# Decoder step with gated feed-forward: seven-product up projection in 18 instead of 9 of 22 slots, all its weight sums on Pool

## The reference, cut to what matters

```python
def conv_ffn(x, buf, p, l):
    u, buf_new = causal_conv(x @ p['ffn_w_up'][l], buf, p['ffn_conv_w'][l])
    u = u + p['ffn_conv_b'][l]
    return (jax.nn.silu(u[..., :D_FF]) * u[..., D_FF:]) @ p['ffn_w_down'][l], buf_new
```

## Time and profile before

| | |
|---|---|
| median of 3 runs | 2889.76 us (2887.61 to 2890.92) |
| the profiled execution | 2890.29 us |
| its span | 2888.6 us |
| PE busy | 2756.4 us, 95% |
| DVE busy | 1524.4 us, 53% |
| ACT busy | 1024.2 us, 35% |
| Pool busy | 477.7 us, 17% |
| mean TensorE clock granted | 0.988 of full speed |

### The profile page before, as it was taken

One profiled execution on the slowest core, in us unless ns is written; L12 is line 12 of the kernel. 1 busy time (PEld: TensorE's weight loads), 2 busy tenths in 40 slices (PEclk: granted clock), 3 DMA queues, 4 the chain that ended last, 5 costly groups with the idle time before them and its releaser, 6 DMA issues. The chain is left out here.

```text
span 2888.6 us, 58689 instructions
## 1 busy us (share of the span) xinstructions
PE 2756.4 (95%) x22859; PEld 2195.5 (76%) x22859; DVE 1524.4 (53%) x3221; ACT 1024.2 (35%) x3105; POOL 477.7 (17%) x605
## 2 busy tenths in 40 slices
PE   7999999999999999999999899899998999999998
PEld 4779768898766667898766777668895679867887
DVE  7665547642243327753542565337726875537661
ACT  2233234522432224431655344325412133324431
POOL 0000110063213210054100002110161000110044
PEclk9999999999999999999999999999999999999998
DMA  5420124434333223343433004533442330123442
GB/s 155 155 75 6 40 71 146 132 127 116 87 108 91 72 78 119 130 132 116 138 104 109 6 6 122 162 113 128 132 137 77 122 105 6 27 68 121 131 136 78
DMA packets 356654, 287.82 MB, mean 100 GB/s; under 512 B 74700, under 2 KB 352764, under 8 KB 355996
## 3 DMA queue, kind: packets, MB, share of 16 engines
q1 hardware_dynamic: 337456, 267.03, 30.1%
q10 hardware_dynamic: 14828, 14.93, 1.6%
q0 software_dynamic: 4096, 2.11, 0.4%
HBM read 263.29 MB, written 20.73 MB: 98 GB/s over the span
## 5 line engine op out<-in xcount | busy, mean ns | idle before, releaser
L362 PE MATMUL bank<-h,weights 128*128 128x320 f32 (+2 forms) x3152 | 788.6, 408 | 8.1 <-ACT h L447 8.1
L362 PEld LDWEIGHTS bank<-h,weights 128*128 128x128 f32 (+1 forms) x3152 | 567.9, 189 | 217.3 <-issue 17.1
L362 PE MATMUL bank<-arena,weights 128*128 128x320 f32 (+5 forms) x3088 | 663.3, 375 | 12.2 <-DVE arena L1407 6.6
L362 PE MATMUL bank<-arena 128*128 128x160 f32 (+7 forms) x5034 | 640.1, 291 | 12.3 <-DVE arena L2745 5.1
L362 PEld LDWEIGHTS bank<-arena,weights 128*128 128x128 f32 (+2 forms) x3088 | 505.4, 188 | 153.3 <-issue 23.0
L362 PEld LDWEIGHTS bank<-arena 128*128 128x128 f32 (+2 forms) x5034 | 543.7, 171 | 37.1 <-issue 14.5
L571 POOL TENSOR_TENSOR arena<-weights 128x512 f32<-128x512 f32 (+1 forms) x48 | 58.2, 1212 | 726.6 <-DMA weights<-ffn_w_down 630.6
L362 PE MATMUL bank<-h,arena 64*64 64x64 f32 (+3 forms) x3000 | 174.4, 232 | 2.6 <-DVE h L1980 1.7
L1643 POOL TENSOR_TENSOR arena<-arena,consts 128x256 f32<-128x256 f32 x30 | 22.9, 765 | 829.1 <-DVE arena L1968 583.9
L362 PEld LDWEIGHTS bank<-h,arena 64*64 64x64 f32 (+1 forms) x3000 | 151.3, 143 | 7.9 <-DVE h L1980 2.8
L894 DVE SCALAR_TENSOR_TENSOR arena<-arena,params 128x336 f32<-128x336 f32 x176 | 105.7, 601 | 68.2 <-ACT arena L754 59.4
(11 more groups left out here) (373 smaller groups left out, 3697.5 us busy)
## 6 DMA issues: line engine op xcount, KB each, us to landing
weights<-ffn_w_up SPq DMA_DIRECT2D x88, 1024.0 KB, 5.1
weights<-ffn_w_down SPq DMA_DIRECT2D x32, 1024.0 KB, 5.4
weights<-rw_wrkv SPq DMA_DIRECT2D x24, 1024.0 KB, 5.2
weights<-gdn_w_in SPq DMA_DIRECT2D x24, 1024.0 KB, 5.4
arena<-cache_mla_latent SPq DMA_DIRECT2D x108, 128.0 KB, 2.3
weights<-ffn_w_down SPq DMA_DIRECT2D x16, 768.0 KB, 4.9
weights<-rw_wo SPq DMA_DIRECT2D x8, 1024.0 KB, 5.5
weights<-gdn_wo SPq DMA_DIRECT2D x8, 1024.0 KB, 5.8
```

Of the source, the lines that this page charges most:

```text
L362: return pe.matmul(out, lhsT, rhs, start=first, stop=last, skip_group_check=True)
```

## The change

Slots 4 to 21 are all of the seven-product kind: 18 per layer instead of 9. Their weight sums all go to Pool, in front of the sums for the down projection on its queue; DVE makes none. DVE's gate is split: in even iterations the two products (L875), in odd ones, for the tiles of the iteration before, the multiplication by the sigmoid (L882 and L884 in the changed file); the HFF mixes move to the odd iterations behind it (7, 9, 15, 17 and 21; the last to 22). The waits on u2, c21 and c12 of the slot two before become waits on the slot before. In the changed file the lines have moved: L898 and L901 are the two convolution steps, L921 u2, L928 tt, L908 and L909 c22 and c12, L943 c21, L581 to L586 the mixes, L570 to L575 the weight sums.

```diff
         UP = [(c, half) for c in range(11) for half in range(2)]
-        FASTS = range(4, 21, 2)
+        FASTS = range(4, 22)
         summed = [key for l in range(layers) for key in
                   [("up", l, UP[s][1], UP[s][0]) for s in FASTS] + [("down", l, c, part) for c in range(4) for part in range(3)]]
...
 
         POOL_SUM = {"m6": "s2", "m5": "s1", "m7": "s3", "m3": "s4"}
-        DVE_SUM = {"m6": "ds2", "m5": "ds1", "m7": "ds3", "m3": "ds4"}
         MIX_FOR = {"m6": "mix2", "m5": "mix1", "m7": "mix3", "m4": "mix4"}
...
                     pe.wait_ge(*at("c22", key))
-                if step in DVE_SUM:
-                    pe.wait_ge(*at(DVE_SUM[step], key))
+                if step in POOL_SUM:
...
                     act.wait_ge(*at("m1", key))
-                    if s - 4 in FASTS:
-                        act.wait_ge(*at("u2", slot_key(l, s - 4)))
-                    act.activation(S1C[s // 2 % 2], of(("fa", key))[:, 0:HN], ACT.Copy).then_inc(*to("s1c", key))
+                    if s - 2 in FASTS:
+                        act.wait_ge(*at("u2", slot_key(l, s - 2)))
+                    act.activation(S1C[s % 2], of(("fa", key))[:, 0:HN], ACT.Copy).then_inc(*to("s1c", key))
                 if s >= 1:
...
 
         def pool_ffn(pool, l):
             pool.wait_ge(*at("rstd", 4 * l + 2))
+            for s in FASTS:
+                half_sums(pool, slot_key(l, s), POOL_SUM)
             for c in range(4):
                 for part in range(3):
...
 
-            def gate(m):
+            def gate_products(m):
 
                 g, u = CONV[:, 0, m % 2, :], CONV[:, 1, m % 2, :]
                 dve.wait_ge(*at("conv", (l, 1, m)))
-                if m:
-                    dve.wait_ge(*at("hff", (l, m - 1)))
-                dve.tensor_tensor(GD[:, 0, :], g, u, ALU.mult).then_inc(*to("gate_gu", (l, m)))
+                if m >= 2:
+                    dve.wait_ge(*at("hff", (l, m - 2)))
+                dve.tensor_tensor(GD[:, m % 2, :], g, u, ALU.mult).then_inc(*to("gate_gu", (l, m)))
+
+            def gated(m):
+
                 dve.wait_ge(*at("gate_gu", (l, m)))
                 dve.wait_ge(*at("gate_s", (l, m)))
-                s = EGATE[:, m % 2, :]
-                dve.tensor_tensor(HFF[:, m, 0:SEQ], GD[:, 0, 0:SEQ], s[:, 0:SEQ], ALU.mult)
-                win = [ap[:, 256:336].rearrange("p (b w) -> p b w", b=DEC)[:, :, 2:10] for ap in (GD[:, 0, :], s)]
+                gu, s = GD[:, m % 2, :], EGATE[:, m % 2, :]
+                dve.tensor_tensor(HFF[:, m, 0:SEQ], gu[:, 0:SEQ], s[:, 0:SEQ], ALU.mult)
+                win = [ap[:, 256:336].rearrange("p (b w) -> p b w", b=DEC)[:, :, 2:10] for ap in (gu, s)]
                 dve.tensor_tensor(sample(HFF[:, m, SEQ:NT]), win[0], win[1], ALU.mult).then_inc(*to("hff", (l, m)))
 
             def conv(n):
...
                     dve.wait_ge(*at("gate_e", (l, m - 2)))
+                    dve.wait_ge(*at("gate_gu", (l, m - 2)))
                 if n:
                     dve.wait_ge(*at("conv", (l, order[n - 1][1], order[n - 1][3])))
...
                     fb, fc, fd = (of((name, key)) for name in ("fb", "fc", "fd"))
-                    if s - 2 in FASTS:
-                        dve.wait_ge(*at("c21", slot_key(l, s - 2)))
+                    if s - 1 in FASTS:
+                        dve.wait_ge(*at("c21", slot_key(l, s - 1)))
                     dve.wait_ge(*at("m6", key))
                     dve.wait_ge(*at("s1c", key))
-                    dve.tensor_tensor(U2, fb[:, 0:HN], S1C[s // 2 % 2], ALU.subtract).then_inc(*to("u2", key))
+                    dve.tensor_tensor(U2, fb[:, 0:HN], S1C[s % 2], ALU.subtract).then_inc(*to("u2", key))
                 conv(2 * s - 1)
                 if key:
                     dve.wait_ge(*at("m5", key))
                     dve.wait_ge(*at("u2", key))
-                    if s - 2 in FASTS:
-                        dve.wait_ge(*at("c12", slot_key(l, s - 2)))
+                    if s - 1 in FASTS:
+                        dve.wait_ge(*at("c12", slot_key(l, s - 1)))
                     dve.tensor_tensor(TT, fc[:, 0:HN], U2, ALU.add).then_inc(*to("tt", key))
                     dve.wait_ge(*at("m7", key))
                     dve.wait_ge(*at("tt", key))
                     last_half(2 * s + 1, "c22", key, fd, TT, ALU.add)
-                if s + 1 in FASTS:
-                    half_sums(dve, slot_key(l, s + 1), DVE_SUM)
                 if s % 2 == 0:
-                    gate(s - 2)
-                    gate(s - 1)
+                    gate_products(s - 2)
+                    gate_products(s - 1)
+                if s % 2 and s > 1 or s == len(UP):
+                    pair = s - 2 if s == len(UP) else s - 3
+                    gated(pair)
+                    gated(pair + 1)
                 if key:
                     dve.wait_ge(*at("m3", key))
                     last_half(2 * s, "c12", key, fb[:, HN:NT], TT, ALU.subtract)
                     dve.wait_ge(*at("m4", key))
                     dve.tensor_tensor(XP[:, (2 * s + 1) % 4, 2:2 + HN], fd[:, 0:HN], U2, ALU.add).then_inc(*to("c21", key))
-                if s % 2 == 0 and s // 2 - 1 in MIXED:
-                    part, a, b = MIXED[s // 2 - 1]
+                if (s % 2 and s > 1 or s == len(UP)) and pair // 2 in MIXED:
+                    part, a, b = MIXED[pair // 2]
                     k0, kp = DOWN_ROWS[part][0], DOWN_ROWS[part][1] // 2
-                    dve.wait_ge(*at("hff", (l, s - 1)))
...
```

More of the change, by code:

```diff
@@ L161 @@
     "fast_weights": "s1 s2 s3 s4",
-    "fast_weights_dve": "ds1 ds2 ds3 ds4",
     "fast_activations": "mix1 mix2 mix3 mix4",
@@ L621, in pe_fast_up @@
                     pe.wait_ge(*at("c22", key))
-                if step in DVE_SUM:
-                    pe.wait_ge(*at(DVE_SUM[step], key))
+                if step in POOL_SUM:
+                    pe.wait_ge(*at(POOL_SUM[step], key))
                 if step in MIX_FOR and (c, half) == UP[FASTS[0]]:
@@ L937, in dve_ffn @@
                     dve.tensor_tensor(XP[:, (2 * s + 1) % 4, 2:2 + HN], fd[:, 0:HN], U2, ALU.add).then_inc(*to("c21", key))
-                if s % 2 == 0 and s // 2 - 1 in MIXED:
-                    part, a, b = MIXED[s // 2 - 1]
+                if (s % 2 and s > 1 or s == len(UP)) and pair // 2 in MIXED:
+                    part, a, b = MIXED[pair // 2]
                     k0, kp = DOWN_ROWS[part][0], DOWN_ROWS[part][1] // 2
-                    dve.wait_ge(*at("hff", (l, s - 1)))
+                    dve.wait_ge(*at("hff", (l, pair + 1)))
                     dve_mixes(dve, [DMIX[part][:, i, a:b] for i in range(4)], HFF[:, k0 + a:k0 + b, :],
-                              HFF[:, k0 + kp + a:k0 + kp + b, :], ("down", l, part, s // 2 - 1))
+                              HFF[:, k0 + kp + a:k0 + kp + b, :], ("down", l, part, pair // 2))
             for c in range(4):
```

## The result

The changed kernel takes **2979.3 us** (median of 4 runs, 2977.72 to 2980.17), the kernel before 2889.3 in runs beside them: a ratio of 1.032, 95% interval 1.0303 to 1.0328. It is 90 us slower; forecast were 53.

A forecast was written before the change was run, and what follows sets the result against it. Up-projection matmuls on PE set the pace now; after the change PE would wait for DVE, held up by Pool's adds. 2890.3 - 36.4 - 3.5 + 92.9 = 2943.3 us, forecast 2943, range 2902 to 2992 (8 in 10).

The forecast's parts named there:

- every add costs in full: Rival: in the up projection each Pool set costs DVE 4.1 us, giving 3000 us; chance 0.20 for 2975 to 3010.
- the walk: Following Pool's adds through DVE's chain per up-phase slot: +92.9 us, forecast 2943 us; chance 0.62 for 2910 to 2975.
- -36.4: PE in the up projection: 36 more slots go from 8.61 to 7.60 us, saving 36.4 us if PE stays the bound.
- -3.5: The 3.5 us that PE already waits for DVE's half of the scheme, subtracted because the new stalls contain it.
- Weight sums cost PE nothing as data: Pool's sums in the up projection are ready with more than a slot of cover, so PE never waits for them.
- The price by the whole length of an add: If each Pool add held DVE for 1.27 us, not 1.0, some 68 us more: an estimate of 3011 us.
- The slots without mixes: DVE's up-phase chain 8.51 us, 0.91 over PE's 7.60, in 52 steps over four layers: 47.3 us.
- The slots behind mixes: DVE's up-phase chain with HFF mixes 10.45 us, 2.85 over PE's 7.60, in 16 steps over four layers: 45.6 us.
- The start of the phase: First up-phase slots: each Pool set was taken to wait for one of three buffers; no separate cost.
- The end of the phase at nothing, ACT at nothing, the gate split at nothing: Phase end hidden by 7.3 us of cover, up to 1 us per layer in the range; ACT's copies and gate split cost nothing.
- The adds hide: Rival: Pool's adds fall where DVE needs no second SBUF input, only mix slots stall; 2874 us, chance 0.12.
- It doesn't do what it says: Rival: up-phase slots wait for Pool's sums, so the nine slots' gain is lost; near 2890 us, chance 0.03.

The follow-up runs named there:

- The four experiments on the sums: Against the changed kernel, up-projection sums dropped (2850.4 us), replaced by unread one-tile adds (2902.6), unread two-input adds (2983.0), or Pool fills (2853.2).
- the kernel without sums: Changed kernel without the 72 sets of up-projection weight sums, PE reading raw weight blocks instead: 2850.4 us in a single run.
- with fills: Changed kernel with PE reading raw blocks and Pool memsets of about an add's length in place of the up-projection adds: 2853.2 us.
- with the sums on DVE: Changed kernel, all 18 slots seven-product and gate split, but every up-phase weight sum on DVE: 2906.8 us, ratio 1.005.
- two apart: Kernel before, with only the weight sums of its nine slots per layer moved from DVE to Pool: 2911.1 us, ratio 1.007.
- one ahead and one beside: Changed kernel with Pool's sets for slots 5 and 6 waiting for m1 of the slot ahead of theirs: 2990.5 us, ratio 1.035.
- the adds at 0.66 us: Changed kernel with PE reading raw blocks and Pool making four unread adds per slot, one tile as both inputs, no waits between: 2902.6 us.
- 12 chosen slots: Kernel before with the gate split and slots 5, 11 and 13 seven-product as well, sums on DVE: 2872.1 us, ratio 0.9945.
- 16 or 18: Gate split, sums on DVE: seven-product slots 4 to 18 and 20, 2881.0 us; all 18 slots, 2906.8 us.

## Why the prediction was right, and where it was not

- **Direction and mechanism: right.** PE waits for DVE and DVE for Pool's reads. The four experiments on the sums leave no other cause.
- **The time: partly luck.** 2979.3 us lies in the band that the prediction gave to the rival "every add costs in full" (2975 to 3010), not in the walk's (2910 to 2975). The mechanism was the walk's, and what brought the time there were two terms that the sum did not have, the start of the phase and the clock. The range held because it had been drawn wide enough for the rival.
- **-36.4: right**, by the slots of 7.61 us in the kernel without sums. The waits behind the -3.5 cost some 4 us of slot time before; the kernel without sums has 6 us of its own at slots 20 and 21, so its total does not prove this term.
- **Weight sums cost PE nothing as data: right.** PE never waits for Pool's sums.
- **The price by the whole length of an add** would be more than the "some 68 us" of the prediction: 4 x 0.27 us in each of 68 slots are 73, which would make 3017 us and not 3011.
- **The slots without mixes: right, slightly high.** 8.40 us instead of 8.51, 0.80 over and not 0.91: a step is held for 0.9, not 1.0. 52 x 0.91 = 47.3 would be 42 at 0.80, but only 36 of the 52 ran so; the 16 behind a mix slot took 9.41.
- **The slots behind mixes: mis-sized, and the clock was missing.** The chain was 10.74 us for a forecast of 10.45, and most of its wait was for u2 in front of m3, where the prediction had only c22 in front of m4. But my sum had PE at full speed right behind a stall. After the 2.1 and 0.4 us in which PE idled, the granted clock fell to its lower level in 15 of the 16 cases, and the next step took some 9.5 instead of 8.40 us. The 16 chains cost 5 us more than forecast, the 16 steps behind them 14 more, the 36 others 3 less: the 17 steps per layer come to 107.8 - 92.9 = 15 us over the forecast.
- **The start of the phase: costed at nothing, measured 28.7 us.** This is the step that failed. I wrote that a set "waits for one of three buffers", which holds in the steady state alone. In the first slots the buffers are free, three sets run back to back, and DVE, and behind it ACT, get late for slot 4. Of the four starts, 19.6 us are waits and 9 the lower clock. That Pool's adds cause it is shown: without them, with fills or with the sums on DVE m4 of slot 4 is on time. That it takes three sets in a row is not: two apart cost 5.3 to 6.8 us, and one ahead and one beside still 5.0. Why DVE has so little slack in front of slot 4 was not tried.
- **The end of the phase at nothing, ACT at nothing, the gate split at nothing: right** at the end and for the split; ACT was not slow itself but passes DVE's delay on to s1c at slot 4.
- **The rivals.** "Every add costs in full" gave 3000 and is ruled out slot by slot (8.40 us, not 9.54, where the clock is at its upper level); the total came between the walk and it for other reasons, the start and the clock. "The adds hide" would need less than 2.16 us exposed per slot; the adds at 0.66 us came near this point, and the kernel then lost little more than in the slots with mixes and at the four starts. "It doesn't do what it says" did not occur.

The sum with the measured terms: 2890.3 - 36.4 - 3.5 + 28.7 + 107.8 = 2986.9, less the 9.2 us by which the rest was shorter: 2977.7, the profiled execution. (The 107.8 was found as what is left, so the sum closes by itself; counted from step to step it is 108.8.)

## What to carry to other kernels

Moving elementwise adds with SBUF inputs to Pool doesn't take them off DVE where DVE's own operations have two SBUF inputs: count per slot how many of them meet Pool's, and compare with the slack that the slot has. Cost the first and the last slots of a phase apart from the steady state: free buffers let a prefetching engine start at once, and the next phase's adds begin before this one ends. A short stall of TensorE costs again by the clock that it gets afterwards, here from under half of the wait to nearly all of it. A total that agrees to a tenth proves little; compare the slots. Where two engines are near their limit, convert only the slots in which both have slack: 12 chosen slots gave more than 16 or 18.

## What was not expected of the hardware

- A Pool add whose two inputs are the same tile held a DVE step for 0.66 us, one with two different inputs, in a chain of waits, for 0.90. The first kind took 1.23 us itself beside DVE, the second 1.31 to 1.53. Which of the two, inputs or waits, makes this wasn't tried.
- Pool fills of the same length hold DVE not at all.
- TensorE's granted clock went to its lower level behind a wait of 3.5 us (m2 to m4 took 6.38 instead of 3.26 us), of 4.9 us, and mostly behind the pair 2.1 + 0.4 us; behind 0.26 + 0.44 us it didn't.
- Between single kernels the parts with the same instructions differed by up to 0.5% of the whole; the cause stays open.
